# Rotary columns from the weights, roots at the evictions, divisions ahead of the side work

## The reference, cut to what matters

```python
h = x @ w_in
c_q, c_kv, k_rope, q_s, k_s, v_s = _split(h, EVEN_SPLIT)      # 384, 256, 32, 512, 128, 128
q = (_rms_norm(c_q, q_norm) @ w_uq).reshape(B, S, 8, 64 + 32)
q_rope = _apply_rope(q[..., 64:], cos, sin)                   # [x1*c - x2*s, x2*c + x1*s]
kv = (_rms_norm(c_kv, kv_norm) @ w_ukv).reshape(B, S, 8, 64 + 64)
k_nope, v = kv[..., :64], kv[..., 64:]
k_rope = _apply_rope(k_rope[:, :, None, :], cos, sin)[:, :, 0]
o_mla = _mla_attend(q_nope, q_rope, k_nope, k_rope, v)        # causal softmax, 8 heads
o_swa = _swa_attend(q_s, k_s, v_s, sinks, rel_bias)           # window of 128, 8 heads
return jnp.concatenate([o_mla, o_swa], axis=-1) @ w_out
```

## Time and profile before

| what | value |
|---|---|
| median of 3 runs | 2377.24 us (2374.42 to 2381.46) |
| the profiled execution | 2373.81 us, its span 2372.0 us |
| TensorE busy, granted clock over the span | 2238.6 us (94%), 0.979 |
| VectorE, ScalarE, GpSimd busy | 1242.3, 894.9, 344.0 us |
| first block's attention, from its first scores | 52.6 to 267.5 us |
| fox, memory, sparse attention | 739 to 937, 1460 to 1527, 1669 to 1757 us |

### The profile page before, as it was taken

One profiled execution on the slowest core, in us unless ns is written; L12 is line 12 of the kernel. 1 busy time (PEld: TensorE's weight loads), 2 busy tenths in 40 slices (PEclk: granted clock), 3 DMA queues, 4 the chain that ended last, 5 costly groups with the idle time before them and its releaser, 6 DMA issues.

```text
span 2372.0 us, 28020 instructions
## 1 busy us (share of the span) xinstructions
PE 2238.6 (94%) x10188; PEld 1748.6 (74%) x10190; DVE 1242.3 (52%) x1955; ACT 894.9 (38%) x1475; POOL 344.0 (15%) x216
## 2 busy tenths in 40 slices
PE   7878899999999998899999998999989997999998
PEld 5646678888876775688888776658768775888886
DVE  4466564244364444553344476377489677443344
ACT  3444443133244444342243253432543343332333
POOL 0000330000340000520001340124023133000001
PEclk9999999999999999999999999999999998999999
DMA  6012223333323222233333233123322142323322
GB/s 168 15 37 61 63 79 99 106 89 98 93 80 96 72 79 73 62 103 101 98 97 98 88 99 102 42 58 94 91 66 67 40 116 63 95 82 114 88 73 72
DMA packets 360370, 196.69 MB, mean 83 GB/s; under 512 B 12592, under 2 KB 355389, under 8 KB 360270
## 3 DMA queue, kind: packets, MB, share of 16 engines
q1 hardware_dynamic: 360270, 195.36, 28.8%
HBM read 193.19 MB, written 2.14 MB: 82 GB/s over the span
## 4 chain that ended last, share of the span: by engine, by line
PE 82%; DVE 10%; ACT 4%; issue 3%; SPq 1%; DMA 0%; POOL 0%; DVEq 0%; ACTq 0%; POOLq 0%
PE PB L394 20%; PE PB L396 20%; PE PB L395 20%; PE PB L1331 2%; PE PB L1333 2%; PE PB L1332 2%; PE PB L495 2%; PE PB L476 2%; PE PB L522 2%; DVE WL L364 1%; PE PB L1412 1%; ACT WH L358 1%; PE PB L1359 1%; PE PB L1239 1%; PE PB L1240 1%
## 5 line engine op out<-in xcount | busy, mean ns | idle before, releaser
L358 ACT ACTIVATE WH<-RAW 128x1024 fp32r<-128x1024 f32 (+2 forms) x367 | 369.5, 1010 | 391.3 <-PE PB L396 359.6
L394 PE MATMUL PB<-XH,WH 128*128 128x512 f32 x1248 | 496.0, 397 | 8.6 <-DVE WL L364 3.1
L396 PE MATMUL PB<-XH,WL 128*128 128x512 f32 x1248 | 490.2, 393 | 0.0
L395 PE MATMUL PB<-XL,WH 128*128 128x512 f32 x1248 | 490.0, 393 | 0.0
L374 DVE TENSOR_TENSOR WL<-RAW,WH 128x1024 fp32r<-128x1024 f32 x192 | 252.8, 1316 | 186.8 <-ACT WH L358 177.0
L394 PEld LDWEIGHTS PB<-XH,WH 128*128 128x128 f32 x1248 | 236.6, 190 | 61.7 <-issue 9.3
L396 PEld LDWEIGHTS PB<-XH,WL 128*128 128x128 f32 x1248 | 235.9, 189 | 51.3 <-issue 0.8
L395 PEld LDWEIGHTS PB<-XL,WH 128*128 128x128 f32 x1248 | 236.5, 189 | 48.8 <-issue 0.8
L364 DVE TENSOR_TENSOR WL<-RAW,WH 128x1024 fp32r<-128x1024 f32 (+3 forms) x135 | 164.5, 1221 | 139.6 <-ACT WH L358 139.2
L396 PE MATMUL PB<-HH,WL 128*128 128x512 f32 x512 | 199.2, 389 | 0.0
L394 PE MATMUL PB<-HH,WH 128*128 128x512 f32 x512 | 199.2, 389 | 0.0
(11 more groups left out here) (508 smaller groups left out, 3730.5 us busy)
## 6 DMA issues: line engine op xcount, KB each, us to landing
RAW<-in_w_up SPq DMA_DIRECT2D x64, 512.0 KB, 4.1
RAW<-in_w_down SPq DMA_DIRECT2D x64, 512.0 KB, 3.9
RAW<-in_w_ffn_gate_up SPq DMA_DIRECT2D x44, 512.0 KB, 3.8
RAW<-in_w_gate SPq DMA_DIRECT2D x32, 512.0 KB, 4.1
RAW<-in_od_w_in SPq DMA_DIRECT2D x24, 512.0 KB, 6.4
RAW<-in_w_in SPq DMA_DIRECT2D x24, 512.0 KB, 3.9
RAW<-in_ple_w_gate SPq DMA_DIRECT2D x16, 512.0 KB, 4.0
RAW<-in_w_ffn_down SPq DMA_DIRECT2D x16, 512.0 KB, 4.0
```

The source lines that it names most:

```text
L358: act.activation(WH[:, s, 0:nb], RAW[:, s, 0:nb], ACT.Copy).then_inc(hi_done[s], 1)
L394: pe.matmul(PB[b][0:m, 0:n], WH[:, s, k, 0:m], rh[:, kk, :], start=kk == 0, stop=False)
L395: pe.matmul(PB[b][0:m, 0:n], WH[:, s, k, 0:m], rl[:, kk, :], start=False, stop=False)
L396: x = pe.matmul(PB[b][0:m, 0:n], WL[:, s, k, 0:m], rh[:, kk, :], start=False, stop=kk == last)
```

## The change

- **Weights.** The tiles of `kr` and `uq` get 32 more columns, the rotary ones with their halves swapped, by two more DMAs for each tile (`load_turned`), with a semaphore `roped` of their own, on which ScalarE's rounding waits. The products of `uq` have 128 outputs instead of 96, `kr` 64 instead of 32. Scores of latent heads are summed over 128 rows: 64 plain, 32 with the cosine, 32 with the signed sine, against a key whose rotated part stands there twice.
- **Latents.** ScalarE applies the gain as it rounds out of PSUM (`n_hi`), VectorE takes the low part out of PSUM. The root of c_q goes, times scale and turn table, into `RQ`, by which VectorE multiplies each `uq` at its eviction; the root of c_kv into `RK`, by which it multiplies the key half of `ukv`, and, turned to tokens by event `rt`, the values at `v4`. `split`, `kswap` and `qswap` are gone; the refining is cut into `root1` and `root2`, and `krot` (4 operations) rotates the key.
- **Evictions.** The key half of `ukv` moves from ScalarE to VectorE.
- **Order.** In `dve_attend` the division of step c+1 stands before `between(c)`, in all four attentions. `QUOTA` and the lists are new; in the latent steps the quota goes 3, 4, 6, 2.
- GpSimd's memset of `KR` goes; the table of constants is 608 columns smaller.

```diff
-    a[64:96, C_COS:C_COS + T] = np.concatenate([np.cos(ang), np.cos(ang)], 1).T
-    a[64:96, C_SIN:C_SIN + T] = np.concatenate([np.sin(ang), np.sin(ang)], 1).T
+    a[0:64, C_TURN:C_TURN + T] = 1.0
+    a[64:96, C_TURN:C_TURN + T] = np.concatenate([np.cos(ang), np.cos(ang)], 1).T
+    a[96:128, C_TURN:C_TURN + T] = np.concatenate([-np.sin(ang), np.sin(ang)], 1).T
...
+            if n in ROPED and per == 0:
+                act.wait_ge(roped[s], ROPED[n])
...
-                pe.wait_ge(sem["qrope"], cnt.value("qrope", ("rot", 2 * g + 1)))
+                evac_of(pe, M_A["uq", 2 * g])
+                evac_of(pe, M_A["uq", 2 * g + 1])
...
             if start:
                 start()
+            dve_normalise(dve, *steps[0])
             for c, (kind, g, qb) in enumerate(steps):
-                dve_normalise(dve, kind, g, qb)
                 if c + 1 < len(steps):
                     dve_max(dve, *steps[c + 1])
                 if qb == 0 and c:
                     dve_out(dve, *steps[c - 1][:2])
+                if c + 1 < len(steps):
+                    dve_normalise(dve, *steps[c + 1])
                 between(c)
...
-        WITH_SWA = [("cq", 0), ("cq", 1), ("cq", 2), ("q", 2), ("ckv", 0), ("var", "cq"), ("ckv", 1), ("split", "cq"), ("q", 3),
-                    ("var", "ckv"), ("kr", 0), ("split", "ckv"), ("uq", 0), ("uq", 1), ("kswap", 0), ("qswap", 0), ("ukv", 0),
-                    ("qswap", 1), ("ukv", 1), ("uq", 2), ("uq", 3), ("qswap", 2), ("qswap", 3)]
+        WITH_SWA = [("cq", 0), ("cq", 1), ("q", 2), ("cq", 2), ("ckv", 0), ("var", "cq"), ("ckv", 1), ("root1", "cq"), ("q", 3), ("root2", "cq"),
+                    ("kr", 0), ("krot", 0), ("var", "ckv"), ("uq", 0), ("root1", "ckv"), ("uq", 1), ("root2", "ckv"), ("uq", 2), ("ukv", 0), ("ukv", 1),
+                    ("uq", 3), ("rt", 0)]
         WITH_MLA = [("v4", 0), ("ukv", 2), ("ukv", 3), ("os", 0), ("v4", 1), ("os", 1)]
-        WITH_MLA += [("uq", 4), ("uq", 5), ("qswap", 4), ("ukv", 4), ("qswap", 5), ("ukv", 5), ("os", 2), ("v4", 2), ("os", 3)]
-        WITH_MLA += [("uq", 6), ("uq", 7), ("qswap", 6), ("ukv", 6), ("qswap", 7), ("ukv", 7), ("os", 4), ("v4", 3)]
-        WITH_MLA += [("os", 5), ("os", 6), ("os", 7)]
-        PIECES = {"cq": 8, "ckv": 8, "q": 8, "kr": 8, "uq": 3, "ukv": 2, "os": 4, "split": 0}
-        QUOTA = [6, 6, 6, 6, 6, 6, 5, 6, 6, 5, 6, 6, 5, 4, 4, 4, 5, 5, 5, 5, 5, 4, 4, 4, 4, 4, 4, 3, 3, 3, 3, 3]
+        WITH_MLA += [("uq", 4), ("uq", 5), ("ukv", 4), ("ukv", 5), ("uq", 6), ("uq", 7), ("v4", 2), ("ukv", 6), ("ukv", 7)]
+        WITH_MLA += [("os", 2), ("os", 3), ("v4", 3), ("os", 4), ("os", 5), ("os", 6), ("os", 7)]
+        PIECES = {"cq": 8, "ckv": 8, "q": 8, "kr": 8, "uq": 3, "ukv": 2, "os": 4, "krot": 0, "root1": 0, "root2": 0}
+        QUOTA = [6, 6, 6, 6, 6, 6, 5, 5, 5, 5, 5, 5, 5, 4, 4, 4, 3, 4, 6, 2, 3, 4, 6, 2, 3, 4, 6, 2, 3, 4, 6, 2]
...
+                sp.dma_start(RAW[:, s, 0:nk, at_:at_ + 16], src[:, :, 16:32]).then_inc(roped[s], 16)
+                sp.dma_start(RAW[:, s, 0:nk, at_ + 16:at_ + 32], src[:, :, 0:16]).then_inc(roped[s], 16)
...
+            pool.wait_ge(sem["kr"], cnt.value("kr", "twice"))
             for h in range(8):
-                x = pool.tensor_copy(K96[64:96, h], KR[64:96, :])
+                x = pool.tensor_copy(KM[64:128, h], KR[64:128, :])
...
-                        yield from lin_parts(pe, st, [8], XH, XL, 32)
+                        yield from lin_parts(pe, st, [8], XH, XL, 64)
...
-                            pe.wait_ge(sem["n_lo"], cnt.value("n_lo", 2))
-                        yield from lin_parts(pe, st, [3], CQH, CQL, 96)
+                            for j in range(3):
+                                evac_of(pe, M_A["cq", j])
+                        yield from lin_parts(pe, st, [3], CQH, CQL)
...
-                    done(act.activation(SQC[:, j] if j < 3 else SQK[:, j - 3], PB[b][:], ACT.Square), "sq", j)
-                    out_of_bank((ACC[:, j], slice(0, P), 1.0))
+                    g = VCOL["ev_q_norm", 0] if j < 3 else VCOL["ev_kv_norm", 0] - 3
+                    done(act.activation(CQH[:, j] if j < 3 else CKH[:, j - 3], PB[b][:], ACT.Copy, scale=VEC[:, g + j:g + j + 1]), "n_hi", j)
+                    done(act.activation(SQC[:, j], PB[b][:], ACT.Square), "sq", j)
+                    nxt()
...
-                    out_of_bank((K96[0:64, i], slice(0, 64), 1.0), (VT[i % 2 * 64:i % 2 * 64 + 64, :], slice(64, 128), 1.0))
+                    done(act.activation(VT[i % 2 * 64:i % 2 * 64 + 64, :], PB[b][64:128], ACT.Copy), "v_half", i)
+                    nxt()
...
-                done(dve.tensor_tensor(tmp[64:96, :], PB[7][64:96, :], SIN, ALU.mult), "misc_free", swap_key)
-                done(dve.tensor_tensor(dst, dst, COS, ALU.mult), "chain_d", ("rc", swap_key))
...
-                done(dve.tensor_tensor(dst, dst, tmp[64:96, :], ALU.add), out_name, out_key)
...
+                    x = dve.scalar_tensor_tensor(lo, PB[b][:], VEC[:, g + j:g + j + 1], hi.bitcast(F32), ALU.mult, ALU.subtract)
+                    x.then_inc(evac[b], 1)
...
+                    done(dve.tensor_tensor(KR[64:128, :], KR[64:128, :], TURN[64:128, :], ALU.mult), "kr", "parts")
...
+                    done(dve.tensor_copy(RTB["cq"][1][64:96, :], KR[96:128, :]), "kr", "moved")
...
+                    done(dve.tensor_tensor(KR[64:96, :], KR[64:96, :], RTB["cq"][1][64:96, :], ALU.add), "kr", "rot")
...
+                    done(dve.tensor_copy(KR[96:128, :], KR[64:96, :]), "kr", "twice")
...
-                    dve.tensor_scalar(Q96[:, i], PB[b][0:96], -(96 ** -0.5), None, ALU.mult).then_inc(evac[b], 1)
+                    dve.tensor_tensor(QM[:, i], PB[b][:], RQ[:], ALU.mult).then_inc(evac[b], 1)
...
+                    dve.tensor_tensor(KM[0:64, i], PB[b][0:64], RK[0:64, :], ALU.mult).then_inc(evac[b], 1)
...
-                    token_major(("v4", i), V4[:, :, i * P:i * P + P])
-                elif what == "var":
-                    rsqrt_dve(dve, i, 384 if i == "cq" else 256, 1e-5, bufs=LATB)
-                    for j in range(3) if i == "cq" else range(3, 5):
-                        g = VCOL["ev_q_norm", 0] if j < 3 else VCOL["ev_kv_norm", 0] - 3
-                        done(dve.scalar_tensor_tensor(ACC[:, j], ACC[:, j], VEC[:, g + j:g + j + 1], LATB[0][:], ALU.mult, ALU.mult), "norm", ("c", j))
...
+                    done(dve.tensor_tensor(V4[:, :, i * P:i * P + P], turned, RT.unsqueeze(2).to_broadcast([P, TT, P]), ALU.mult), "misc_free", ("v4", i))
...
+                elif what == "root1":
+                    r, v, q = RTB[i]
+                    dve.wait_ge(sem["rs_ln"], cnt.value("rs_ln", i))
+                    done(dve.tensor_scalar(v[:], PB[7][:], 1.0 / (384 if i == "cq" else 256), 1e-5, ALU.mult, ALU.add), "misc_free", ("var", i))
+                    dve.wait_ge(sem["rs_exp"], cnt.value("rs_exp", i))
+                    done(dve.tensor_tensor(q[:], r[:], r[:], ALU.mult), "chain_d", ("n1", i))
+                    dve.wait_ge(sem["misc_free"], cnt.value("misc_free", ("var", i)))
+                    dve.wait_ge(sem["chain_d"], cnt.value("chain_d", ("n1", i)))
+                    done(dve.scalar_tensor_tensor(q[:], q[:], -0.5, v[:], ALU.mult, ALU.mult), "chain_d", ("n2", i))
+                elif what == "root2":
+                    r, v, q = RTB[i]
+                    dve.wait_ge(sem["chain_d"], cnt.value("chain_d", ("n2", i)))
+                    done(dve.scalar_tensor_tensor(r[:] if i == "cq" else RK[:], q[:], 1.5, r[:], ALU.add, ALU.mult), "rsq", i)
+                    dve.wait_ge(sem["rsq"], cnt.value("rsq", i))
+                    if i == "cq":
+                        done(dve.scalar_tensor_tensor(RQ[:], TURN[:], -(96 ** -0.5), r[:], ALU.mult, ALU.mult), "rsq", "turned")
```

More of the change, by code:

```diff
@@ L108, in program @@
         used = [ctx.enter_context(nc.semaphore(f"used{s}")) for s in range(4)]
+        roped = [ctx.enter_context(nc.semaphore(f"roped{s}")) for s in range(4)]
         evac = [ctx.enter_context(nc.semaphore(f"evac{b}")) for b in range(2)]
@@ L159, in program @@
         CST = region("CST", [P, C_A - 384], F32)
+        RQ = region("RQ", [P, T], F32)
         latent_at = top[0]
@@ L818, in program @@
         misc_keys = ["bandv", "vec", "vec2", "vs", *[("bandt", k) for k in range(4)]]
-        misc_keys += [ev if ev[0] != "kswap" else "kswap" for ev in WITH_SWA + WITH_MLA if ev[0] in ("var", "kswap", "qswap", "v4")]
+        misc_keys += [ev for ev in WITH_SWA + WITH_MLA if ev[0] in ("var", "rt", "v4")]
+        ROPED = {}
+        for c, ev in enumerate(TILES_A):
+            if ev[0] in ("kr", "uq"):
+                ROPED[c] = 32 + max([0] + [ROPED[n] for n in ROPED if n % 4 == c % 4])
+        V_HELD = {M_A["ukv", i] + 2: i for i in range(8)}
         misc_keys += [
@@ L1578, in fill @@
                 for what, i in events:
+                    if what in ("krot", "root1", "root2"):
+                        continue
```

(2 more changed lines are left out.)

118 lines of the change are left out of this document (56 added, 62 removed).

## The result

The changed kernel takes **2343.2 us** (median of 4 runs, 2341.0 to 2345.1) against 2375.8 for the kernel before, run beside it (4 runs, 2373.7 to 2381.5). The ratio is 0.986, 95% interval 0.985 to 0.988: 33 us less. Forecast were 2334 us and a gain of 43. The time lies in the range (2320 to 2354) and just above the narrow forecast (2327 to 2341). The gain is made of larger pieces than forecast, less one loss that no term had. The profiled execution after took 2343.3 us, its span is 2341.3.

What follows compares the result with a forecast made beforehand. TensorE, busy 2238.6 of 2372.0 us, was taken as the bound. First block 35.6 us plus fox 2, memory 4 and sparse 1.6 summed to 43 us, so 2334 us from the median; range 2320 to 2354.

Steps and rivals of the forecast that it cites:

- Terms 1 and 2: First block: TensorE's waits for division and rotation go, 28.6 us at most, and the half clock behind them, 8.5 us.
- Term 3: First block: nine float32 swap products leave TensorE, four root transposes come in; net 7.3 us gained.
- Term 4: First block: VectorE's edits leave it 13 us lighter; not itself a gain in the sum.
- Term 5: Attention steps: divisions put first fall into VectorE's 36.1 us gap before remainders, mostly without delaying what stood behind.
- Term 6: First block, steps 11 to 15: VectorE runs late; TensorE stands 4.3 us, plus 1.5 us of half clock.
- Term 7: First block's latent steps 20 to 28: late ukv 5 evictions and exponentials cost 3 us in all.
- Rival B: The walk is too dark: no new wait anywhere, gain 53 us, 2324 us; chance 0.13.
- Term 8: Other attentions, new order only: fox gains 2 us, memory 4, sparse 1.6.
- rival C: All four attentions: the early division holds VectorE, up to 96 us over 80 steps, 2430 us; chance 0.05.
- A: First block: VectorE stays the bound, half of the waits and half clocks stay; gain 29 us, 2348 us; chance 0.22.
- D: First block: small loads are late, ScalarE waits on them, 43 us eats the gain, 2377 us; 0.05 with anything near no change.

Runs made afterwards that it cites:

- order alone: The kernel before with nothing but the divisions put first in each step: 2364.2 us, ratio 0.995.
- work alone: The changed kernel with the divisions back at the end of each step, so only the rotary and root part: 2348.6 us, ratio 0.989.
- early table load: The changed kernel plus one tiny ScalarE tanh after the eighth index product's eviction, bringing the gate's table load forward: 2327.05 us, ratio 0.979.
- two edits of the last wait: On the changed kernel with the tanh table loaded early: ukv 0 and 1 ahead of uq 2, 2326.8 us; key rotation moved to GpSimd, 2326.6 us.
- halved loads: The changed kernel with each of the 18 swapped-column loads split into two halves of 64 partitions: 2344.1 us, ratio 0.986.

## Why the prediction was right, and where it was not

**Terms 1 and 2, waits and the half clock behind them.** Right in kind. TensorE's idle time in the stage fell from 30.1 us to 6.3, by 23.8; terms 1, 6 and 7 together said 21.3. Half clock while TensorE was busy cost 9.5 us before (19.0 us of busy time, in five places) and 1.7 after, in one place. So 7.8 us went, where terms 2 and 6 left 7.0. (The windows of the earlier trace rows miss 12 us of clock, but 2.5 of them fell while TensorE stood and cost nothing.)

**Term 3, swaps.** What is left of the 42.2 us is 42.2 - 23.8 - 7.8 = 10.6 of work, forecast 7.3 (the term's own sum is off: nine times 0.9 is 8.1 us, not 7.9). Counted from each start to the next one, with time at half clock counted half, the nine swaps held TensorE 6.2 us and the root's transposes 0.3. The other 4.6 us are in products that are not fewer, the small transposes of the probabilities (17.5 to 14.2 us) and the small products that add the mask (3.5 to 2.2). Behind a wait the four transposes at 115.7 us hold TensorE 0.66 us, the four at 60.2 us, without one, 0.41, both at full clock. So a wait seems to cost a little more than its idle time, and no term had that; for the mask products the reason is open. That `uq` with 128 columns costs TensorE nothing held: its 24 products of `CQH` with `WH` took 5.9 us before and 6.1 after.

**Term 4, VectorE's edits.** The multiplication with a broadcast column takes 0.68 us, as the copy did; 0.7 was taken, with twice that as the bound. VectorE's busy time in the stage fell by 11.1 us (127.05 to 115.93, by the windows), 13 forecast.

**Term 5, divisions first.** Right: the gap before `WL` took them, 36.1 us to 4.2. The order alone shortens the first block by 21.2 us.

**Term 6, what is late next.** The wait of 2.8 us before the first latent scores stands to a tenth where it was put, and its half clock costs 1.7 us in the profiled run (1.5 forecast). But the reason was too wide: VectorE's surplus was counted over steps 11 to 15, and the rotation moved to GpSimd shows that only the last two or three of these steps count, since VectorE idles ahead of them. Of the other 1.5 us 0.8 came, in a wait for the eviction of a q (`QM`) 6 us earlier.

**Term 7, the latent steps.** Forecast 3 us; measured 0.9, for an exponential. The evictions of `ukv` 5 were not late.

First block: **42.2 against 35.6**. Rival B's 44.4 was nearer, though by luck: waits of 2.8, 0.9 and 0.8 us did come, and what made up for them, the shorter small products, B did not have either.

**Term 8, the other attentions.** Fox 3.1 (2 forecast); the waits for the division fell from 5.8 us in 12 places to 3.5 in 4. Memory 5.8 (4 forecast): both waits of the earlier trace rows went, with a half clock behind one of them (0.83 in 1470 to 1480 us before) that the term had left out. Sparse **-1.4 (1.6 forecast), wrong in sign**. TensorE's waits there, from 1700 us:
```profile
PE PB L1336 <- DVE YAL L633: 4.5, 1, 4.5
PE PB L397 <- DVE WL L367: 4.2, 1, 4.2
```
The wait for `YAL` stayed, as forecast. The wait for the division of 2.8 us went, and one of 4.2 for a remainder came. VectorE's timeline shows rival C's mechanism, in this one place:
```profile
1704.39 1.28 DVE L575 TENSOR_REDUCE STAT<-PB 128x1 f32<-128x512 f32 x2
1709.31 0.16 DVE L602 RECIPROCAL STAT<-STAT 128x1 f32<-128x1 f32 x1 [3.63 <-ACT PR L593]
...
1710.96 4.52 DVE L367 TENSOR_TENSOR WL<-RAW,WH 128x1024 fp32r<-128x1024 f32 x2
```
The division, now first, holds VectorE for 3.63 us until the exponentials of 512 columns end, and behind it stand two remainders of 2.3 us each that TensorE needs. The order alone shows this wait too (4.3 us), the work alone does not. The step that failed is "pays two waits for exponentials in its middle": the price of a wait there was taken as that of the short steps, and what was queued behind it was not named. As a whole C was wrong; over the kernel the order gains.

**What no term had.** "Sum: 35.6 + 2 + 4 + 1.6" takes everything outside the attentions as it was. The pieces measured 42.2 + 3.1 + 5.8 - 1.4 = 49.7, the index stretch took 20.3. Removing time ahead of a stretch moves it against whatever the clock is granted by; this is the mis-sized part of the forecast, and it is larger than the error of any term. Without it the gain would have been some 46 us: the changed kernel with two extra index products stands at 2329.8, less their 1.0 us at 2328.8, and before it at 2375.2. That the forecast of 43 came near the measured 33 is in part luck: the pieces were 6.5 us larger than their terms, and the 20.3 that no term had went the other way.

**Rivals A and D.** A's signs (evictions `QM` and `KM` over 10 us) came to 3.6; its sum has a slip, 26.6 for 35.6 - (18.6 - 8.8) = 25.8, which moves its time of 2348 by less than 1 us. D's did not come at all: the 18 small DMAs are hidden, and 18 more as well. My estimate by the fixed part that the Trainium skill gives (DMA: Bandwidth & Descriptors, "Anatomy of one DMA") was 36 us if nothing hid them. The page gives it for DMAs issued by GpSimd, and these are SyncE's, which landed in 1.9 us at 24 KB. The trace had 30 us of lead, and the trace decided.

A kernel better than both is the changed one with the early table load: 2327.05 us, 16 below the changed kernel and 49 below the one before (ratio to before 0.979, where the changed kernel has 0.986). The two edits of the last wait bring nothing on top.

## What to carry to other kernels

Where one engine's divisions, remainders and evictions share a queue, put the operation that the bound engine waits for first if the others behind it have idle time anyway; look then at the last and largest step, where what stands behind it may be what is needed. Read the granted clock not only where the change is: here a wait of 1.0 us in a stretch of small products cost 16 us of the kernel's time, and an unrelated shift of one microsecond switched that on or off. Such a wait is worth removing even when it shows only 1 us. A change that measures 20 us off its terms should be looked up in the clock of untouched stretches before its terms are doubted.

## What the hardware showed that was not expected

The clock can stay at 1.2 GHz for about 50 us while TensorE is busy without a gap (10 of 10 us in each window), in a stretch that alternates index products of 64 rows with groups of three or six full products. In the four traces that show it (the changed kernel, the one with halved loads, the order alone, the kernel before with two extra products) it fell 1.6 to 1.75 us behind the end of a wait of 1.0 us; in six other kernels the same wait did nothing.

What ends it is open: in three of the four it lasted about 51 us, past the last index product, and in the order alone 27 us, while index products still went on. What the place of the wait is measured against was not worked out.

The Trainium skill (TensorE: Matmul & The Clock Gate, "What's actually happening") says that the monitor behind the clock runs freely and does not start with the kernel. The runs show that a shift of about 1.0 us decides. But a monitor that is free of the kernel's start should let runs of one kernel differ, and here all runs of a kernel had the same outcome. The time since the span's start is not the measure: in the kernel before with two extra products the wait ends at 1545.78 us and sets off the half clock, in the kernel before itself at 1545.54 and does not, since the two executions differ by a few tenths of a us already at the first scores (52.1 and 52.6). By its advice under "Why this matters for your kernels" a wait this short would do no harm; here it cost 20 us in its stretch, and the measurement decides.

The same sensitivity shows on a small scale in the first block. The changed kernel and the one with the early table load run the same instructions up to 1480 us, and both have the wait of 2.8 us before the latent scores. Two windows behind it, of the changed kernel and then of the other:
```profile
140.00:142.00 2.00, 2.00 (x6) 1.52 (x5) 0.90 (x4) 1.98 (x7) 0.00 (x0) 0.50 0.00 1
```
```profile
140.00:142.00 2.00, 2.00 (x12) 1.68 (x10) 1.24 (x6) 1.84 (x7) 0.00 (x0) 1.00 0.35 100
```
0.50 in one and 1.00 in the other, and the latent part takes 87.3 us and 85.7. Yet in the index stretch a kernel seems to keep to one of the two outcomes from run to run: the mean clocks of a kernel's runs agree to 0.003. Why it is so stable there is open.
